# Cached keys and indexer keys laid out dimension first, page by page, in a one-step hybrid decoder layer

## What is computed

```
q, k, v, iq, ik, iw, ... = split(x @ w_in)
ik_past = cache_idx_k[page_table]            # (8 sequences, 512 past, 64)
s  = einsum('bqhd,bkd->bqhk', iq, concat(ik_past, ik)) * 64 ** -0.5    # 16 indexer heads
sc = einsum('bqhk,bqh->bqk', relu(s), iw * 16 ** -0.5)
sel = top_k(sc, 130)                         # for each new token
logits = q . k_sel * 128 ** -0.5 - slope * distance   # keys from cache_k by page, 8 heads, 2 key heads
attn = softmax(logits) @ v_sel
```

## Time and profile before

| | us |
|---|---|
| median of three runs | 1671.73 |
| profiled execution | 1673.12 |
| its span, first to last instruction | 1671.3 |
| TensorE busy (matmul) | 1632.1 (98%) |
| VectorE busy | 678.4 (41%) |
| ScalarE busy | 429.2 (26%) |
| GpSimd busy | 609.5 (36%) |
| all transfers | 174.35 MB, 104 GB/s over the span |

### The profile page before, as it was taken

How to read it: one execution, slowest core, us unless ns; L and a number is a source line. 1 busy time by engine, 2 the same in 40 slices (tenths; PEclk the granted TensorE clock), 3 DMA queues, 4 the chain that set the end, 5 groups by cost and what they waited for, 6 DMA issues and landing times.

```text
span 1671.3 us, 28144 instructions
## 1 busy us (share of the span) xinstructions
PE 1632.1 (98%) x10993; PEld 1518.4 (91%) x10993; DVE 678.4 (41%) x1624; ACT 429.2 (26%) x531; POOL 609.5 (36%) x182
## 2 busy tenths in 40 slices
PE   8999999999999999999999999999999999999995
PEld 6888489999999988899999999999999999988884
DVE  4022877432112101114888788706572222210018
ACT  4222622232332113221111221222361221231120
POOL 4244023432323232344544444555343333343330
PEclk9999899999999999999999999999999999999998
DMA  7333042233233443632223232233336444542213
GB/s 247 95 101 84 14 131 76 76 97 91 72 98 100 139 112 100 174 92 76 77 77 96 76 86 77 77 97 104 90 87 187 130 122 132 192 147 80 96 51 113
DMA packets 247373, 174.35 MB, mean 104 GB/s; under 512 B 17963, under 2 KB 224267, under 8 KB 246395
## 3 DMA queue, kind: packets, MB, share of 16 engines
q1 hardware_dynamic: 242635, 163.25, 34.3%
q10 hardware_dynamic: 4608, 9.44, 1.5%
HBM read 156.75 MB, written 16.63 MB: 104 GB/s over the span
## 4 chain that ended last, share of the span: by engine, by line
PE 94%; DVE 3%; issue 1%; ACT 1%; SPq 1%; POOL 0%; DMA 0%; DVEq 0%; POOLq 0%; ACTq 0%
PE ps L1531 72%; PE ps L1518 11%; PE ps L1574 2%; PE ps L1728 1%; PE ps L1737 1%; PE ps L1684 1%; PE ps L1515 1%; PE ps L1586 1%; PE ps L1514 1%; PE ps L1883 1%; DVE y L1478 1%; DVE y L1484 1%; PE ps L1702 1%; DVE bias L1185 1%; SPq L508 0%
## 5 line engine op out<-in xcount | busy, mean ns | idle before, releaser
L687 POOL TENSOR_TENSOR wlo<-raw,whi 128x2048 fp32r<-128x2048 f32 x115 | 531.2, 4619 | 901.7 <-ACT whi L778 901.7
L1531 PE MATMUL ps<-xhi,whi 128*128 128x288 f32 (+2 forms) x2912 | 648.5, 300 | 3.2 <-ACT tmp_tanh L984 2.2
L1531 PE MATMUL ps<-xlo,whi 128*128 128x288 f32 (+2 forms) x2912 | 646.4, 300 | 0.0
L1531 PE MATMUL ps<-xhi,wlo 128*128 128x288 f32 (+2 forms) x2912 | 642.4, 298 | 0.4 <-issue 0.4
L1531 PEld LDWEIGHTS ps<-xhi,whi 128*128 128x128 f32 x2912 | 470.9, 188 | 8.8 <-issue 2.5
L1531 PEld LDWEIGHTS ps<-xhi,wlo 128*128 128x128 f32 x2912 | 471.7, 188 | 3.0
L1531 PEld LDWEIGHTS ps<-xlo,whi 128*128 128x128 f32 x2912 | 471.4, 188 | 2.9
L778 ACT ACTIVATE whi<-raw 128x2048 fp32r<-128x2048 f32 x115 | 219.4, 1908 | 161.1 <-PE ps L1515 125.6
L1518 PE MATMUL ps<-whi,mixed 128*128 128x512 f32 x512 | 158.1, 390 | 0.5 <-POOL wlo L767 0.5
L1518 PEld LDWEIGHTS ps<-whi,mixed 128*128 128x128 f32 x512 | 95.8, 188 | 22.2 <-POOL wlo L767 1.8
L1369 DVE SCALAR_TENSOR_TENSOR ps<-U,dwT,ps 128x256 f32<-128x256 f32 x232 | 112.6, 485 | 0.0
(11 more groups left out here) (277 smaller groups left out, 1188.0 us busy)
## 6 DMA issues: line engine op xcount, KB each, us to landing
raw<-in_w_in_dram SPq DMA_DIRECT2D x83, 1024.0 KB, 5.7
raw<-in_w_o_dram SPq DMA_DIRECT2D x16, 1024.0 KB, 5.2
both_gates<-gates_dram SPq DMA_DIRECT2D x16, 576.0 KB, 6.7
raw<-in_w_att_out_dram SPq DMA_DIRECT2D x16, 512.0 KB, 4.2
raw<-in_w_conv_out_dram SPq DMA_DIRECT2D x16, 512.0 KB, 5.5
gates_dram<-tmp_gate ACTq DMA_DIRECT2D x24, 288.0 KB, 2.1
vpage<-in_cache_v_dram SPq DMA_DIRECT2D x32, 128.0 KB, 2.1
kpage<-in_cache_k_dram SPq DMA_DIRECT2D x32, 128.0 KB, 2.1
```

The lines of the kernel that those rows point to most:

```text
L687: nc.gpsimd.tensor_tensor(wlo[:, buf, 0:width], raw[:, buf, 0:width], whi[:, buf, 0:width].bitcast(F32), ALU.subtract).then_inc(lo_ready, 1)
L1531: ins = mm(ps[:, bank + half, 0:width], w[b][:, k, :], x[:, k, t0 + half * width:t0 + (half + 1) * width], start=(k == k0 and m == 0), sto ...
```

## The change

The host hands over cache_k as (page, key head, dimension, token) and cache_idx_k as (page, dimension, token). The loads then write keys and indexer keys with the dimension on partitions, and the transposes, ScalarE's copies and their semaphores are gone. idx_kT holds all eight sequences in four places: even sequences in partitions 0 to 63, odd ones in 64 to 127. iq_new follows that with four smaller copies per gather in place of two, and without the memset. The products of two sequences, each over 64 rows, stand one after the other in TensorE's list, then two sums follow. Their results rotate through three pairs of PSUM banks. kTs takes the room of kpage; SyncE waits for logits where it waited for transposes, and no longer waits before the indexer pages of sequences 4 to 7. The wait for tile_taken ahead of the key stages goes. The declarations of semaphores are left out below.

```diff
@@ -181,7 +181,8 @@
     rep_c = at("rep_c", [P, 3 * P], F32, B0 + HB + 16384)
-    idx_page = at("idx_page", [P, 4, PAGES, 2, IDIM], F32, B0)
+    idx_kT = at("idx_kT", [P, DB // 2, PAST], F32, B0)
@@ -205,12 +206,11 @@
     pT = at("pT", [P, GROUP, 4 * P], F32, S0 + 12000)
-    kTs = at("kTs", [P, 2, PAST], F32, S0 + 12000 + 4096)
...
     q_last = at("q_last", [P, HEADS * LAST], F32, R0 + 4736)
-    iq_new = at("iq_new", [P, DB, 2, IH // 2 * DS], F32, S0 + 13088)
+    iq_new = at("iq_new", [P, DB // 2, 2, IH // 2 * DS], F32, S0 + 13088)
@@ -233,10 +233,9 @@
     relus = at("relus", [P, 4, 4 * P], F32, M0 + 3488)
-    idx_kT = at("idx_kT", [P, 2, PAST], F32, M0 + 3488)
...
     probs_last = at("probs_last", [P, LP], F32, M0 + 3488)
-    kpage = at("kpage", [P, 2, PAGES, 2 * DH], F32, M0 + 3488)
+    kTs = at("kTs", [P, 2, KVH, PAST], F32, M0 + 3488)
@@ -418,6 +413,9 @@
+        def idx_bank(v):
+            return (2048, 3072, 1024)[v % 3]
@@ -501,13 +499,11 @@
             def load_idx(b):
-                if b >= 4:
-                    sp.wait_ge(idx_turned, b - 3)
+                half = slice(64 * (b % 2), 64 * (b % 2) + 64)
...
                     v = page(b, n)
-                    sp.dma_start(idx_page[:, b % 4, n, :, :],
-                                 cache_idx_k[ds(v, 1), :, :].rearrange("a t (o d) -> (a t) o d", o=1)
-                                 .broadcast_to([P, 2, IDIM])).then_inc(idx_here[b % 4], 16)
+                    sp.dma_start(idx_kT[half, b // 2, n * P:(n + 1) * P],
+                                 cache_idx_k[ds(v, 1), :, :].rearrange("a d t -> (a d) t")).then_inc(idx_here[b % 4], 16)
@@ -564,8 +560,8 @@
                     v = page(b, n)
-                    sp.dma_start(kpage[:, b % 2, n, :], cache_k[ds(v, 1)].rearrange("a t g d -> (a t) (g d)")
-                                 ).then_inc(kpage_here[b % 2], 16)
+                    sp.dma_start(kTs[:, b % 2, :, n * P:(n + 1) * P], cache_k[ds(v, 1)].rearrange("a g d t -> d (a g) t")
+                                 ).then_inc(kTs_here[b % 2], 16)
@@ -588,11 +584,11 @@
-                sp.wait_ge(kTs_out, 4 * k)
+                sp.wait_ge(s_logits, 4 * k)
-            sp.wait_ge(kTs_out, 12)
+            sp.wait_ge(s_logits, 12)
@@ -605,7 +601,7 @@
-            sp.wait_ge(kTs_out, 2 * DB)
+            sp.wait_ge(s_logits, 2 * DB)
@@ -869,16 +865,12 @@
             for v in range(2 + DB):
-                n, o = (LP if v < 2 else LS), 2048 + 1024 * (v % 2)
+                n, o = (LP if v < 2 else LS), idx_bank(v)
...
                                      ).then_inc(relu_ready, 1)
-                if v < DB:
-                    act.wait_ge(idx_turned, v + 1)
-                    nc.scalar.activation(idx_kT[:, v % 2, :], ps[:, 2 + v % 2, :], ACT.Copy).then_inc(idx_kT_ready, 1)
@@ -928,16 +920,6 @@
-            def within_pair(s):
-                if s in S_NEW:
-                    for u in range(4 * S_NEW.index(s), 4 * S_NEW.index(s) + 4):
-                        act.wait_ge(kTs_out, u + 1)
-                        if u >= 2:
-                            act.wait_ge(s_logits, u - 1)
-                        nc.scalar.activation(kTs[:, u % 2, :], ps[:, 2 + u % 2, :], ACT.Copy).then_inc(kTs_ready, 1)
@@ -961,8 +943,6 @@
-                    if b == 1:
-                        within_pair(s)
@@ -1149,7 +1129,6 @@
-            link(nc.vector.memset(iq_new[:, :, :, :], 0.0))
@@ -1166,9 +1145,10 @@
                 for par in range(2):
-                    half = slice(64 * par, 64 * par + 64)
-                    ins = nc.vector.tensor_copy(iq_new[half, :, par, DS * j:DS * j + DS],
-                                                iqT[half, j, LP:TOK].rearrange("p (b t) -> p b t", b=DB))
+                    new = iqT[64 * par:64 * par + 64, j, LP:TOK].rearrange("p (b o t) -> p o b t", o=2, t=DS)
+                    for odd in range(2):
+                        ins = nc.vector.tensor_copy(iq_new[64 * odd:64 * odd + 64, :, par, DS * j:DS * j + DS],
+                                                    new[:, odd, :, :])
@@ -1632,39 +1612,32 @@
-            def turn_idx(b):
-                pe.wait_ge(idx_here[b % 4], 16 * PAGES * (b // 4 + 1))
-                if b >= 2:
-                    pe.wait_ge(idx_kT_ready, b - 1)
-                for n in range(PAGES):
-                    ins = nc.tensor.transpose(ps[:, 2 + b % 2, n * P:n * P + P],
-                                              idx_page[:, b % 4, n, :, :].rearrange("p c d -> p (c d)"), ident)
-                ins.then_inc(idx_turned, 1)
...
-                o = 2048 + 1024 * (v % 2)
-                pe.wait_ge(relu_ready, HEAD_UNITS if v < 2 else HEAD_UNITS + v - 1)
+                o = idx_bank(v)
+                pe.wait_ge(relu_ready, HEAD_UNITS if v < 3 else HEAD_UNITS + v - 2)
...
                     b = v - 2
-                    pe.wait_ge(idx_kT_ready, b + 1)
-                    lhs = iq_new[:, b, :, :].rearrange("p c t -> p (c t)")
-                    mm(ps_t[:, o:o + PAST], lhs, idx_kT[:, b % 2, :], start=True, stop=True)
-                    ins = mm(ps_t[:, o + PAST:o + LS], lhs, ik_new[:, DS * b:DS * b + DS], start=True, stop=True)
+                    half = slice(64 * (b % 2), 64 * (b % 2) + 64)
+                    pe.wait_ge(idx_here[b % 4], 16 * PAGES * (b // 4 + 1))
+                    lhs = iq_new[half, b // 2, :, :].rearrange("p c t -> p (c t)")
+                    mm(ps_t[:, o:o + PAST], lhs, idx_kT[half, b // 2, :], start=True, stop=True)
+                    ins = mm(ps_t[:, o + PAST:o + LS], lhs, ik_new[half, DS * b:DS * b + DS], start=True, stop=True)
...
             pe.wait_ge(iq_new_ready, IH // 2)
             idx_products(0)
+            idx_products(1)
             for v in range(2 + DB):
-                if v < DB:
-                    turn_idx(v)
-                if v + 1 < 2 + DB:
-                    idx_products(v + 1)
+                if v % 2 == 0 and v + 2 < 2 + DB:
+                    idx_products(v + 2)
+                    idx_products(v + 3)
@@ -1679,17 +1652,10 @@
-                u, rows, at0 = 2 * b + g, slice(32 * (b % 4), 32 * (b % 4) + 32), LP + DS * b
-                pe.wait_ge(kTs_ready, u + 1)
-                mm(ps[rows, 4 + g, :], q_new[:, g, b, :], kTs[:, u % 2, :], start=True, stop=True)
+                rows, at0 = slice(32 * (b % 4), 32 * (b % 4) + 32), LP + DS * b
+                mm(ps[rows, 4 + g, :], q_new[:, g, b, :], kTs[:, b % 2, g, :], start=True, stop=True)
...
                    ).then_inc(s_logits, 1)
-            def turn_keys(b, g):
-                for n in range(PAGES):
-                    ins = nc.tensor.transpose(ps[:, 2 + g, n * P:n * P + P],
-                                              kpage[:, b % 2, n, g * DH:(g + 1) * DH], ident)
-                ins.then_inc(kTs_out, 1)
@@ -1785,21 +1751,15 @@
                         pe.wait_ge(q_new_ready, HEADS)
-                    pe.wait_ge(tile_taken, N_GT + 2 * s - C_OF + 2)
...
                     for c in range(2):
-                        pe.wait_ge(kpage_here[c], 16 * PAGES * (k + 1))
-                    turn_keys(b, 0)
-                    turn_keys(b, 1)
+                        pe.wait_ge(kTs_here[c], 16 * PAGES * (k + 1))
...
                         pe.wait_ge(rep_taken, k // 2 + 1)
-                    logits_new(b, 0)
-                    turn_keys(b + 1, 0)
-                    logits_new(b, 1)
-                    turn_keys(b + 1, 1)
-                    logits_new(b + 1, 0)
-                    logits_new(b + 1, 1)
+                    for c in range(2):
+                        logits_new(b + c, 0)
+                        logits_new(b + c, 1)
@@ -1935,6 +1895,9 @@
+    arrays["in_cache_k_dram"] = _np.ascontiguousarray(_np.transpose(inputs["cache_k"], (0, 2, 3, 1)))
+    arrays["in_cache_idx_k_dram"] = _np.ascontiguousarray(_np.transpose(inputs["cache_idx_k"], (0, 2, 1)))
```

More of the change, by code:

```diff
@@ L301, in build @@
         idx_here = [sem(f"idx_here{i}") for i in range(4)]
-        idx_turned = sem("idx_turned")
-        idx_kT_ready = sem("idx_kT_ready")
         idx_out = sem("idx_out")
@@ L332, in build @@
         rep_taken = sem("rep_taken")
-        kpage_here = [sem("kpage_here0"), sem("kpage_here1")]
+        kTs_here = [sem("kTs_here0"), sem("kTs_here1")]
         vpage_here = sem("vpage_here")
         v_new_here = sem("v_new_here")
-        kTs_out = sem("kTs_out")
-        kTs_ready = sem("kTs_ready")
         s_logits = sem("s_logits")
```

## The result

| | us, median | runs | ratio to before, 95% interval |
|---|---|---|---|
| before, beside it | 1672.47 (1670.78 to 1673.45) | 4 | |
| changed kernel | 1649.79 (1646.00 to 1650.51) | 4 | 0.9861 [0.9846, 0.9876] |
| the same once more | 1649.96 (1647.19 to 1650.61) | 4 | 0.9859 [0.9844, 0.9874] |

The change takes 22.7 us off, where the forecast had 13.3. The measured 1649.8 lies under the forecast of 1658.4 and under the low end of its range, 1652.5. The direction was right, the size was wrong.

A forecast was written before the change was run, and what follows sets the result against it. TensorE's work, 94% of the span, was taken as the bound. Terms -12.5 - 4.6 - 0.5 + 1.0 + 0.6 + 2.7 = -13.3 us from 1671.73 gave 1658.4 us; 8-in-10 range 1652.5 to 1665.

The forecast's parts named there:

- What bounds the kernel: Whole kernel: TensorE's work is 94% of the span, so time leaving its list shortens the kernel unless something else comes due.
- Units one behind the other: Four key stages: four logits units in sequence and one entry take 3.85 us (third stage 3.75), saving 12.5 us in all.
- What the pairs give: Indexer stage: only the small product overlaps the next large one, 0.1 us for each of five pairs, saving 0.5 us.
- rival 3: Indexer stage: product pairs run truly side by side, five products of 1.0 us vanish, 4.5 more than forecast, 1653.9; chance 0.06.
- Indexer stage, what goes: Indexer stage: removed transposes save 3.8 us and one late transfer 0.8 us, sum 4.6 us.
- Change of array height: Indexer stage: ten changes between 64-row and 128-row matmuls cost about 0.1 us each, +1.0 us, bounds 0.3 and 2.0.
- The clock: Indexer stage: first full-height sum comes 2.5 us later, the clock returns half of that later, +0.6 us.
- Rivals 1 and 2: 1: clock at 0.50 to end of indexer stage, 1673 us, chance 0.12; 2: from the heads on, about 1680, chance 0.04.
- Rival 2: Clock falls already in the head stage and stays low to the indexer stage's end, about 1680 us; chance 0.04.
- Gather: VectorE before the indexer stage: 16 more copies filling iq_new at 0.17 us each, +2.7 us, bounds 1.2 and 3.4.
- What becomes late in place of the waits: Key stages: transfers of next keys, values and weight tiles stay early enough for TensorE; nothing charged.
- The reserve: Weight tile starting at 718.06: low part ends 8.6 us early, stages take 5.9, leaving 2.7 us at the least.

The follow-up runs named there:

- first profile: First profiled execution of the changed kernel, unaltered; span 1647.3 us, indexer stage 18.51 us long, all at granted clock 1.00.
- second profile: Profiled execution when an unaltered kernel was run once more; for the changed kernel median 1649.96 us, with 10.24 us at granted clock 0.50 from 194.98.
- the keys alone: Kernel before with only the new layout of cache_k, its loads, semaphores and four logits units in a row; indexer as before; 1653.91 us.
- the products in turn: Changed kernel with TensorE waiting for each even sequence's product before issuing the odd one's (five waits), key units left side by side; 1657.91 us.

## Why the prediction was wrong, point by point

**What bounds the kernel: right.** 98% of the span is TensorE, before and after. Of the 25.8 us gained by the end of the fourth key stage, 24.0 arrive at the end of the kernel in the first profile, the rest going to the new wait and a low stretch.

**Units one behind the other: the step that failed.** "Four units and one entry come to 3.85 us" was the key term; the stage takes 2.89, and four stages save 16.3 us, not 12.5. The trace before showed no two units next to each other, as a group of transposes always stood between, except the last two of a stage, both on the same columns. I took the length of a unit alone (0.99 us) and did not ask whether two on different columns would overlap. Forced into turn they take the forecast's 3.8 again, so the size of a unit was right and its neighbourhood was missed. This step alone is worth 3.8 us.

**What the pairs give: the same mistake, seen and decided wrongly.** What rival 3 said of the pairs was the truth, at 0.06. The argument against it was that the small product "stands between the two large ones" in the list. The large product of the other half starts before the small one all the same. The Trainium skill, page TensorE: Matmul & The Clock Gate, Part 3, The mechanism, calls matmuls strictly in order; the records here show starts in another order (202.1 and 202.5 above), and the measurement decides. By the Trainium skill, page TensorEngine Tiling (Array Packing), Key Properties, tiles operate independently, which is what happened. Four of five pairs take 1.1 to 1.2 us instead of 2.0: 3.3 us instead of 0.5, at full clock, and more of it where the clock is low (4.8 in turn against side by side, waits included). The fifth goes in turn for its relu, which rival 3 had overlooked: it had 5.0.

**Indexer stage, what goes: right.** No transposes, no late transfer. With the low stretch in the stage in both (10.15 and 9.80 us of it), the stage goes from 30.66 us (193.03 to 223.69, second profile of the kernel before) to 22.68, 8.0 less. The forecast's terms for it without the clock give 4.1 (4.6 + 0.5 - 1.0). The overlap of the pairs explains 2.8 to 4.3 of the 3.9 between. The 0.8 us for a late transfer was the figure of one execution: TensorE waited 0.68 us for it there, 0.16 in the second profile and 1.98 with the keys alone.

**Change of array height: right in size, wrong in number.** From the small products to the first sum it is 0.22 us (202.55 to 202.77), between kinds of the same height 0.10 (203.69 to 203.79): 0.1 for a change. In the other direction, from a sum to a product, it is 0.19 (201.40, not shown, to 201.59), again 0.1 more. But the forecast counted ten changes, and the new order makes seven, since the first two pairs of products follow each other and nothing of full height stands before them. The old order had three already, around the products of the last prompt rows. So four were added, 0.4 us and not 1.0.

**The clock: wrong in size, and it is not one number.** I added 0.6 for a clock that comes back later. In the first profile the low stretch was out of the stage, which gives back some 4 us (22.68 against 18.51), and a small one came at 883, after a wait of 2.19 us for tmp_tanh. It costs 1.5 us: the 50 records after that wait take 8.46 us here and 6.93 in the second profile, which has no low stretch there. In the second profile the low stretch was in the stage as before, and not longer. Rivals 1 and 2 did not come: in no profile of the changed kernel did the low clock last beyond 10.24 us in the stage. Rival 2's fall inside the heads did come, for 6.83 us, but cost nothing. With the products in turn the low clock lasted for 20.48 us.

**What the 9.4 us beyond the forecast are made of.** Five of the eight timed runs of the changed kernel have the granted clock of the second profile (0.991) and its time (1649.6 to 1650.6), so I compare the second profiles. There the keys give 3.8 more than forecast and the indexer stage 4.5 (8.0 where the terms with the clock gave 3.5), less 0.1 for the gather and 0.3 for the new wait. That makes 7.9. Another 0.7 is the median before, 1672.47 beside the change and 1671.73 when I forecast. The 0.8 left is less than what one stretch of 3.4 us at 0.50 costs. So the clock is no large part of the difference. How the low stretches fell in the runs that were not profiled is argued, not shown, and nothing here sets the clock.

**Gather: right.** Forecast 2.7, measured 2.81 (heads from 29.37 us, 163.87 to 193.24, to 32.18). A copy of half the columns is hardly shorter, as argued.

**What becomes late in place of the waits: one miss.** I followed the weights and keys as far as TensorE, which never waits for them. I did not follow what stands behind the weights on ScalarE. ScalarE idles 8.24 us for them before it comes to the exponentials, and the normalisation on VectorE then falls under GpSimd's low part from near its start: 0.85 us lost at the transposes of the probabilities (0.3 in the second profile). The reserve was also smaller than argued. GpSimd's low part now ends at 691.16 and the tile starts at 693.16, which is 2.0 us and not 2.7 or more.

## What to carry to other kernels

Before you price matmuls one behind the other, write down which rows and columns of the array each takes: neighbours in the list that share neither can cost the time of one, a small product between them is no bar, and an order by which neighbours differ is free. Such an overlap is gained only if both are ready together; a semaphore between them takes it away. When TensorE's list gets shorter, follow a transfer that comes less early than TensorE to everything that stands behind it on the engines between. On a VectorE that sets the pace count instructions before elements, and look for an engine that idles in front of the stage.

## What the runs showed of the hardware that was not expected

- A VectorE TENSOR_SCALAR on 128x520 fp32 takes 0.49 us alone and 4.03 or 2.21 under GpSimd's 4.6 us TENSOR_TENSOR, and ends 0.29 us after it in both cases. Placed ahead of it, it takes 0.49. By the Trainium skill, GPSIMD Engine Reference, Specifications, GpSimd shares its SBUF interfaces with VectorE, with contention for instructions in a 2-port mode or with two SBUF inputs. The trace agrees that the two get in each other's way, and shows more than a slowdown: the operation does not end until GpSimd's has. No row shows in which mode it ran.
- Matmuls on different rows (64-row halves) or different columns (groups of 32) start out of the order of the list, the large ones of both before the small one of either, where both are ready together.
- The place of a stretch at 1.2 GHz differs between executions of the same instructions: the same stage took 18.51 and 22.68 us.
- A semaphore wait on the product just before costs 0.2 to 0.3 us beyond the work itself (594.62 to 594.88, 216.11 to 216.50).
